# Three edits to a one-core hybrid decoder layer: first feed-forward pair ended tile by tile, an output-projection tile begun early, head norms spread over levels

## Time and profile before

| | us |
|---|---|
| median of 3 runs | 1313.35 (1312.7 to 1317.45) |
| the profiled execution's own time | 1313.02 |
| its span, first to last instruction | 1311.3 |
| TensorE busy (matmul) | 1269.4 |
| VectorE, ScalarE, GpSimd busy | 672.2, 437.3, 322.9 |

### The profile page before, as it was taken

One profiled execution on the slowest core, in us unless ns is written; L12 is line 12 of the kernel. 1 busy time (PEld: TensorE's weight loads), 2 busy tenths in 40 slices (PEclk: granted clock), 3 DMA queues, 4 the chain that ended last, 5 costly groups with the idle time before them and its releaser, 6 DMA issues.

```text
span 1311.3 us, 20499 instructions
## 1 busy us (share of the span) xinstructions
PE 1269.4 (97%) x8200; PEld 1229.8 (94%) x8200; DVE 672.2 (51%) x1126; ACT 437.3 (33%) x580; POOL 322.9 (25%) x195
## 2 busy tenths in 40 slices
PE   7999999999899999989999999999999999999997
PEld 7988879998889899989999999999999999999996
DVE  6786775656698546645454211355451124554334
ACT  5411112223547414643333200333331023333325
POOL 5200000000000044133333322233333223333653
PEclk9999999998999999989999999999999999999999
DMA  7431223425415500011112211111121101112212
GB/s 268 123 95 43 81 68 125 146 63 156 114 51 186 222 1 17 1 50 50 35 48 65 64 48 33 33 49 49 34 72 43 51 29 50 49 50 59 71 44 87
DMA packets 67883, 95.74 MB, mean 73 GB/s; under 512 B 23328, under 2 KB 47904, under 8 KB 67816
## 3 DMA queue, kind: packets, MB, share of 16 engines
q1 hardware_dynamic: 67824, 94.93, 23.6%
HBM read 75.54 MB, written 18.37 MB: 72 GB/s over the span
## 4 chain that ended last, share of the span: by engine, by line
PE 88%; DVE 6%; issue 3%; ACT 2%; POOL 1%; DMA 0%; ACTq 0%; SPq 0%; DVEq 0%; POOLq 0%
PE psum L1119 62%; PE psum L1409 6%; PE psum L1316 5%; PE psum L1189 4%; PE psum L1262 3%; PE psum L1240 1%; DVE SC L1725 1%; PE psum L1236 1%; PE psum L1224 1%; DVE K L1715 1%; DVE QP L1716 1%; DVE XL L1548 1%; PE psum L1200 1%; PE psum L1290 1%; PE psum L1291 1%
## 5 line engine op out<-in xcount | busy, mean ns | idle before, releaser
L1119 PE MATMUL psum<-XH,wh 128*128 128x344 f32 x1485 | 325.5, 328 | 16.5 <-DVE wl L1548 8.5
L1119 PE MATMUL psum<-XL,wh 128*128 128x344 f32 x1485 | 317.1, 322 | 0.0
L1119 PE MATMUL psum<-XH,wl 128*128 128x344 f32 x1485 | 315.2, 321 | 0.0
L1119 PEld LDWEIGHTS psum<-XH,wh 128*128 128x128 f32 x1485 | 249.6, 190 | 22.1 <-DVE XL L1548 9.8
L1119 PEld LDWEIGHTS psum<-XL,wh 128*128 128x128 f32 x1485 | 253.1, 190 | 0.0
L1119 PEld LDWEIGHTS psum<-XH,wl 128*128 128x128 f32 x1485 | 249.3, 189 | 0.0
L1913 DVE SCALAR_TENSOR_TENSOR hb<-ub,cp,hb 128x1024 f32<-128x1024 f32 x44 | 56.5, 1285 | 238.5 <-ACT hb L924 238.5
L1055 POOL TENSOR_TENSOR wl<-raw,wh 128x1024 fp32r<-128x1024 f32 (+1 forms) x44 | 115.7, 2630 | 256.2 <-ACT wh L928 227.1
L923 ACT ACTIVATE ub<-psum 128x1032 f32<-128x1032 f32 x44 | 45.5, 1034 | 206.1 <-PE psum L1119 151.7
L1916 DVE SCALAR_TENSOR_TENSOR hb<-ub,cp,hb 128x1024 f32<-128x1024 f32 x44 | 86.3, 1961 | 1.6
L1058 POOL TENSOR_TENSOR AL<-hb,AH 128x1032 f32 (+1 forms) x22 | 53.3, 2423 | 106.7 <-ACT AH L935 106.7
(11 more groups left out here) (310 smaller groups left out, 1944.4 us busy)
## 6 DMA issues: line engine op xcount, KB each, us to landing
raw<-in_w_up SPq DMA_DIRECT2D x44, 512.0 KB, 3.6
raw<-in_w_units SPq DMA_DIRECT2D x15, 512.0 KB, 4.6
raw<-in_w_dn SPq DMA_DIRECT2D x16, 448.0 KB, 3.4
fscr<-st SPq DMA_DIRECT2D x10, 516.0 KB, 2.9
R<-in_xT SPq DMA_DIRECT2D x8, 516.0 KB, 6.6
out_yT<-R SPq DMA_DIRECT2D x24, 172.0 KB, 1.9
raw<-in_w_dn SPq DMA_DIRECT2D x8, 512.0 KB, 3.6
WOR<-in_w_out SPq DMA_DIRECT2D x6, 512.0 KB, 6.9
```

Source lines behind the costliest of these rows:

```text
L1119: ins = nc.tensor.matmul(psum[:, 3 * slot + b, 0:CW], w, x[:, k, CW * b:CW * b + CW], start=(first and p_ == 0), stop=(last and p_ == 2))
```

## The change

`AHEAD` names the rows 4, 5, 6, 7, 0, 1, 2 of the output projection. A new step "ahead" multiplies row tile 2, block 0, with these seven rows (21 matmuls), into the bank that the last head's second sum of squares has used; `out_group(0)` then adds only row 3. For this the halves of WOR[0] are made behind the last head's output (`wh2 wl2` further ahead in TAIL). All groups now take the rows in the order of AHEAD and then row 3. The norm blocks of heads 0 and 2 (`fin`) are three steps f0, f1, f2 of their own: those of head 0 behind levels 5, 6 and 7 of head 1, those of head 2 behind levels 3, 4 and 4 of head 3; those of head 1 stay together. In the slots of head 2, "1 o save 1" becomes "2 o save". In the first feed-forward pair the products go (s 0, block 0) with the mean inside it, (s 1, block 0), (s 0, block 1) with the variance inside it, (s 1, block 1) and (s 0, block 2) in turn by row, then (s 1, block 2); each tile reports its end by itself. ScalarE splits the next weights of this pair ahead of emptying PSUM, and SyncE issues both weight loads of every pair ahead of the two loads of cp.

```diff
--- before.py
+++ after.py
@@ -60,6 +60,7 @@
 SQ_SLOTS = 6
 LOW_AFTER = 2
 OUTS = [(m, b) for b in range(NB) for m in range(2, KD)]
+AHEAD = [*range(HEADS, KD), *range(HEADS - 1)]
 
 
 def unit_of(kind, h):
@@ -94,11 +95,11 @@
 ]
 SLOTS = [
     ("1 1", "2", "2", "2 load+ 1", "2 s0", "sig+ 2 vb", "2 a+ 1", "2 b+"),
-    ("2 kt", "1 kv 1", "1 o save 1", "1 ms0 1 load+ ms1", "1 s0 ms2 1", "1 vb sig+ fin 1", "1 a+ 1 y", "2 b+"),
-    ("2 kt x gelu0", "1 kv 1 gl0 gelu1", "1 o save 1 gl1 gelu2", "1 ms0 load+ ms1 gl2 gelu3", "1 s0 ms2 1 q3 gl3", "1 vb sig+ fin glu 2", "1 a+ 1", "1 b+"),
-    ("1 kt 1", "1 kv 1 mld0", "2 o save", "1 ms0 1 ms1", "1 s0 1 ms2 mld1 fin", "2 z out 2 zh 1 zl mld2 wload", "1 vb mix0 1 ml0 mix1", "1 ml1 mix2 1 ml2"),
+    ("2 kt", "1 kv 1", "1 o save 1", "1 ms0 1 load+ ms1", "1 s0 ms2 1", "1 vb sig+ f0 1", "1 f1 a+ 1 y", "f2 2 b+"),
+    ("2 kt x gelu0", "1 kv 1 gl0 gelu1", "2 o save gl1 gelu2", "1 ms0 load+ ms1 gl2 gelu3", "1 s0 ms2 1 q3 gl3", "1 vb sig+ f0 f1 f2 glu 2", "1 a+ 1", "1 b+"),
+    ("1 kt 1", "1 kv 1 mld0", "2 o save", "1 ms0 1 ms1 f0", "1 s0 1 ms2 mld1 f1 f2", "2 z out 2 zh 1 zl mld2 wload", "1 vb mix0 1 ml0 mix1", "1 ml1 mix2 1 ml2"),
 ]
-TAIL = "kt 1 kv 2 o save rload 2 ms0 1 ms1 1 f30 m30 ms2 1 f31 l30 m31 f32 p30 l31 m32 wh2 wh3 l32 wl2 p31 p32"
+TAIL = "kt 1 kv 2 o save rload wh2 wl2 2 ms0 1 ms1 1 f30 m30 ms2 1 f31 l30 m31 f32 ahead p30 l31 m32 wh3 l32 p31 p32"
 
 def order():
 
@@ -145,14 +146,18 @@
             o.append(("vb", h))
         elif step in ("kt", "kv", "o"):
             o.append((step, h - 1))
-        elif step == "fin":
-            o.extend([("fin", h - 1, b) for b in range(NB)])
+        elif step in ("f0", "f1", "f2"):
+            o.append(("fin", h - 1, int(step[1])))
         elif step[:2] in ("f3", "m3", "l3"):
             o.append(({"f": "fin", "m": "mix", "l": "ml"}[step[0]], HEADS - 1, int(step[2])))
         elif step[:2] == "p3":
             while queue:
                 put(PART)
             o.append(("last", int(step[2])))
+        elif step == "ahead":
+            while queue:
+                put(PART)
+            o.append(("ahead", 0))
         elif step == "save":
             o.append(("save", h - 1))
             if h < HEADS:
@@ -275,6 +280,12 @@
 
 
 USES = bank_uses()
+AHEAD_BANK = USES[("ms", HEADS - 1, 1)][0]
+
+
+def out_bank(i):
+
+    return i % 6 if i else 6 + AHEAD_BANK
 
 
 class Lane:
@@ -660,6 +671,7 @@
                 def pair(i, first=False):
                     for s in range(2):
                         load_weights(n0 + 2 * i + s, s, w_up[bass.ds(2 * (j0 + i) + s, 1)].rearrange("a p n -> p (a n)"), KD * P)
+                    for s in range(2):
                         conv_params(j0, i, s, first)
                     if not first:
                         store_cache(j0 + i - 1)
@@ -919,14 +931,17 @@
                         elif s == 0:
                             act.wait_ge(halo, 1)
                             act.wait_ge(x1_lo, KD * NB)
+                        if first:
+                            act.wait_ge(loaded[s], 16 * (n0 // 2 + i + 2))
+                            act.activation(wh[s][:, :], raw[s][:, :], ACT.Copy).then_inc(hi_done, 1)
                         act.wait_ge(cp_in[s], 16 * (j0 + i + 1))
                         act.activation(b3(ub[s][:, 2:2 + T]), banks(s), ACT.Copy).then_inc(u_full, 1)
                         act.activation(b3(hb[s][:, :]), banks(s), ACT.Identity, scale=cp[s][:, 2:3], bias=cp[s][:, 3:4]).then_inc(evac[s], 1)
 
-                        if not last:
+                        if not last and not first:
                             act.wait_ge(loaded[s], 16 * (n0 // 2 + i + 2))
                             act.activation(wh[s][:, :], raw[s][:, :], ACT.Copy).then_inc(hi_done, 1)
-                        else:
+                        elif last:
                             act.wait_ge(loaded[s], 16 * (n0 // 2 + i + 2))
                             act.activation(wh[s][:, 0:nk * P], raw[s][:, 0:nk * P], ACT.Copy).then_inc(hi_done, 1)
                     act.wait_ge(conv_done, 2 * (j0 + i) + 2)
@@ -1146,6 +1161,15 @@
                 def done(self, ins):
                     ins.then_inc(fill[self.b], 1)
 
+            def out_rows(i, rows):
+                m, b = OUTS[i]
+                for k in rows:
+                    w_h, w_l = (w[m - 2][:, k * P:(k + 1) * P] for w in (WOH, WOL))
+                    for p_, (w, x) in enumerate(((w_h, XH), (w_h, XL), (w_l, XH))):
+                        last = nc.tensor.matmul(psum[:, out_bank(i), 0:CW], w, x[:, k, blk(b)],
+                                                start=(k == AHEAD[0] and p_ == 0), stop=(k == HEADS - 1 and p_ == 2))
+                return last
+
             pe.wait_ge(x_lo, 1)
             for step in ORDER:
                 kind, c = step[0], step[1]
@@ -1180,6 +1204,10 @@
                     last = product(0, HEADS - 1, XH, XL, c, False, True)
                     if c == NB - 1:
                         last.then_inc(mm_done, 1)
+                elif kind == "ahead":
+                    pe.wait_ge(*freed(("ms", HEADS - 1, 1)))
+                    pe.wait_ge(wo_lo, 1)
+                    out_rows(0, AHEAD)
                 elif kind == "values":
                     cols = slice(c * P, c * P + P) if c < NC else slice(TP, T)
                     u = Use((kind, c, ""))
@@ -1303,18 +1331,17 @@
 
             def out_group(i):
                 m, b = OUTS[i]
-                bank = i % 6
                 if b == 0:
                     pe.wait_ge(wo_lo, m - 1)
-                if i < 6:
-                    pe.wait_ge(*evacuated(OUT_N + i // NB))
+                if i == 0:
+                    pe.wait_ge(m_lo, HEADS)
+                    last = out_rows(0, [HEADS - 1])
                 else:
-                    pe.wait_ge(out_evac, i - 5)
-                for k in range(KD):
-                    w_h, w_l = (w[m - 2][:, k * P:(k + 1) * P] for w in (WOH, WOL))
-                    for p_, (w, x) in enumerate(((w_h, XH), (w_h, XL), (w_l, XH))):
-                        last = nc.tensor.matmul(psum[:, bank, 0:CW], w, x[:, k, blk(b)],
-                                                start=(k == 0 and p_ == 0), stop=(k == KD - 1 and p_ == 2))
+                    if i < 6:
+                        pe.wait_ge(*evacuated(OUT_N + i // NB))
+                    else:
+                        pe.wait_ge(out_evac, i - 5)
+                    last = out_rows(i, AHEAD + [HEADS - 1])
                 last.then_inc(out_done, 1)
 
             def mean_x1(b):
@@ -1370,18 +1397,23 @@
                         pe.wait_ge(x1_lo, KD * b + (k + 1 if b == NB - 1 else KD))
                         return product(s, k, XH, XL, b, k == 0, k == KD - 1)
 
-                    for b, s in ((0, 0), (0, 1), (1, 0), (1, 1)):
-                        for k in range(KD):
-                            first(s, k, b)
-                        if (b, s) == (0, 0):
+                    for k in range(KD):
+                        first(0, k, 0)
+                        if k == 3:
                             mean_x1(NB - 1)
-                        if (b, s) == (1, 0):
+                    for k in range(KD):
+                        first(1, k, 0)
+                    for k in range(KD):
+                        first(0, k, 1)
+                        if k == 2:
                             variance_x1(NB - 1)
                     for k in range(KD):
-                        for s in range(2):
-                            last = first(s, k, NB - 1)
-                            if k == KD - 1:
-                                last.then_inc(mm_done, 1)
+                        first(1, k, 1)
+                        last = first(0, k, 2)
+                    last.then_inc(mm_done, 1)
+                    for k in range(KD):
+                        last = first(1, k, 2)
+                    last.then_inc(mm_done, 1)
                     a = 1
                 with pe.Fori(a, nk) as i:
                     pair(i)
@@ -1849,7 +1881,7 @@
                 dve.wait_ge(out_done, i + 1)
                 dve.wait_ge(r_in[m], 16)
                 r = R[:, m, blk(b)]
-                me(STT(r, r, ALPHA, psum[:, i % 6, 0:CW], ALU.mult, ALU.add), out_evac)
+                me(STT(r, r, ALPHA, psum[:, out_bank(i), 0:CW], ALU.mult, ALU.add), out_evac)
 
             def center_x1(b):
                 dve.wait_ge(mean1, b + 1)
```

## The result

| | before | after |
|---|---|---|
| median, us (range, runs) | 1313.05 (1312.7 to 1317.45, 4) | 1295.07 (1294.41 to 1295.78, 4) |
| profiled execution, its span | 1313.02, 1311.3 | 1294.7, 1293.0 |
| ratio, 95% interval | | 0.9856 [0.9834, 0.9877] |

The prediction was 1297.3 us, in a range of 1292.8 to 1303.5. The gain is 18.0 us by the medians and 18.3 us between the profiled executions, where 15.7 were forecast.

A forecast was written before the change was run, and what follows sets the result against it. TensorE, with matmuls over 97% of the span, was taken as the bound, leaving its waits and clock to gain from. Terms 5.1 + 1.0 - 1.7 + 4.9 + 6.4 = 15.7 off 1313.02 gave 1297.3 us, range 1292.8 to 1303.5.

The forecast's parts named there:

- Part 1: Head 0's norm blocks spread over head 1: shorter wait for QP and clock staying up, gain 5.1 us.
- Part 2: Head 2's norm blocks spread: TensorE's 1.1 us wait for a low half shrinks, gain 1.0 us.
- Part 3: "2 o save" in head 2's slots: longer wait ahead of level 4, low clock behind it, cost 1.7 us.
- What remains is the clock: Head 2's level 4: low clock taken to follow the wait of at least 2.2 us, cost 1.7 us.
- Part 4: Last head's tail: 21 early matmuls of row tile 2 fill TensorE's hole, gain 4.9 us.
- Part 5: First feed-forward pair: TensorE no longer waits for the next low half, nor runs slowly, gain 6.4 us.
- cost nothing: SyncE in the feed-forward: both weight loads ahead of the cp loads cost nothing, buffers being free long before.
- The clock staying up: Rival: clock does not fall at head 2's "2 o save" hole; 1295.6 us, chance 0.2.
- The feed-forward chain: Rival: block 2's last low half in the first pair stays at 555.5; 1301.2 us, chance 0.11.
- no new wait took part 4's place: Rival: tile 3's low half on VectorE slips, opening a hole with low clock; 1300.6 us, chance 0.08.
- part 1 was not void: Rival: spreading head 0's blocks gains nothing, the wait reappearing at the next level; 1302.4 us, chance 0.07.
- cp was never late: Rival "slower": late cp loads hold ScalarE's evacuation in 21 feed-forward pairs, 1 us each; 1318 us, chance 0.02.

The follow-up runs named there:

- the first and third experiment: First: changed kernel with head 0's norm blocks together again, 1302.12 us; third: changed kernel with that and "1 o save 1" put back, 1301.13 us (one run).

## Why the prediction came out as it did

The total was right within its range, and by a sum of terms of which two were wrong.

- **Part 1** (5.1 forecast): 5.2 measured. The wait fell from 2.46 to 0.39 us, as worked out, and the clock stayed up. Two small errors cancelled: the stretch behind the wait gave back 3.1 us instead of 3.4, and the 0.4 us of new waits did not come.
- **Part 2** (1.0): 1.1. The reversal gave the wait of 1.1 back; what its stretch lost beyond that, 1.6 us, was clock.
- **Part 3** (-1.7): 0. The step that failed is "What remains is the clock", which it took to fall behind the longer wait, at a cost of 1.7. It fell, for a stretch of the size taken, but before level 4 and not behind it, so that it filled the hole it was to follow. The step before it held in its cause, that ScalarE's chain sets the Ln; the wait was 0.99 us, not the 2.2 or more forecast, because TensorE came late, not because the Ln came soon. What I left out is that a slow stretch in front of a wait costs nothing. Where the part's place did matter, with the GLU block later, it cost 2.9 us and not 1.7. That the part itself is paid back at level 7 was right: the wait of 1.3 us there is gone.
- **Not in the sum** (0): 1.6 us, from a low clock behind the wait of 2.3 us in head 1's output. I knew of that wait and took it only into the range, as one that the change leaves alone. It does leave the wait alone (2.32 and 2.33 us), yet not the clock behind it. Such falls are in all three profiled executions with head 0's blocks together (before, and the first and third experiment), and in none of the nine others that have this wait. That it goes with the edit is shown, both ways round, in the profiled executions (the others were not seen by stretch); by what is not. The edit also moves this wait 4.7 us earlier in the execution, and the runs do not tell that from the effect of the gap upstream.
- **Part 4** (4.9): 4.8. The 21 matmuls fit the hole. Their reversal costs 3.3 us in a trace whose clock stayed up; the other 1.5 us are the low clock of the kernel before.
- **Part 5** (6.4): 6.0, of which 4.5 up to the second pair (4.8 forecast) and 1.5 of clock (1.65). The last low half came 2.2 us sooner relative to the start, where 2.4 were taken, the hole was 0.76 us instead of 1, and the split began 0.8 us behind that low half, where 0.4 was taken; GpSimd's low half took 2.4 us instead of 2.7. One sentence was wrong in its weight: that the weight loads ahead of the cp loads "cost nothing". That is true, but without them the split ahead of the copies makes ScalarE wait 8 us; the edit is what makes its neighbour possible.

**The rivals.** The clock staying up (1295.6 us) came nearest in time, and not by its mechanism. The clock fell behind waits of 2.47 and 2.26 us, and in the changed kernel where no wait stood directly ahead. By the Trainium skill ("TensorE: Matmul & The Clock Gate", section "HAM oscillation — how this bites in real kernels") only gaps longer than these re-throttle the array; these traces disagree. But the length of the wait does not decide it the other way either: behind waits of 3.18, 2.27 and 2.83 us in the feed-forward the clock stayed at 1.00, and behind one of 3.11 it fell. So the prediction's inference from two falls, that a wait of over 2.4 us is followed by one, is not a rule in these traces. The feed-forward chain moved, no new wait took part 4's place, part 1 was not void, and cp was never late.

The wrong terms, -1.7 for 0 and 0 for 1.6, make 3.3 us; the smaller errors (parts 1, 2, 4 and 5, together 0.2) and the start of head 1's level 6, which comes 0.5 us later, take back 0.7. The spans show the rest: 18.3 less 15.7 is 2.6. Both wrong terms erred to the same side, and the range held because it had been drawn to take in a clock that stays up.

**Left open.** What makes the clock fall at a place and not at another. All seven profiled executions with "2 o save", head 0's blocks spread and the GLU block in its place have a low stretch between 342 and 348 us, and neither of the two with those blocks spread and the part in its old place has one. An execution with "2 o save" and the clock up there was not seen, so the hole at its full size was not measured in this kernel.

## What to carry to other kernels

Price a low clock, like any other delay, by what ends the next wait: in front of a wait for another engine's chain it uses up slack, and where nothing waits behind it, about half its length is paid (2.9 us of 6.9 with the GLU block later). Where a wait of some 2 us is left alone by a change upstream, put the clock behind it into the sum as a term with both ends, since an edit upstream turned it on or off here. A group of edits that looks like one good one and its decoration should be taken apart from the far end too: here the split of the weights ahead of the copies was worth about 2 us with the loads' new order, and without that order the kernel lost 3 us.

## What the runs showed that was not expected

- The same wait, 2.33 us for VectorE's scores in head 1's output, was followed by a clock of about half in three of three profiled executions and by full clock in nine of nine, according to whether the gap of 2.47 us in head 1's level 7, some 25 us earlier, was there (the two kernels with the GLU block later have a wait of 0.9 us in this place).
- The clock fell with no wait directly ahead: to 0.51 from 344.0 to 347.4 us in the changed kernel, 5 us behind the wait of 2.33 us, and to about half from 392.8 to 396.2 us with the GLU block later and the part back. The other kernel with the GLU block later and the one with head 2's blocks together fell in that second place, too. In all of these the last work was the 16 matmuls of a single column and the level's of 64 columns; but the same work in head 2's output was followed by full clock in the other eleven traces.
- Waits of 3.18, 2.27 and 2.83 us in the feed-forward were followed by full clock, one of 3.11 us there by 0.55.
- Nine executions of the kernel before on one chip gave 1312.9 to 1313.9 us at a mean clock of 0.990, 1314.9 to 1318.0 at 0.986 or 0.987, and once 1320.7 at 0.984. The spread goes with the clock; in which stretches it fell in the longer ones was not seen.
